# A two-block model on one core: the mixing part of the second block rearranged

## The reference

```
h = x + 0.5 * swiglu(rms(x))
p = rms(h) @ w_in;  u_conv, q, k, v, q_mem = split(p, [768, 1152, 1280, 1408])
y_conv = conv(u_conv)              # a * sigmoid(gate), 31 causal taps per channel
                                   # (384 channels), + bias, layer norm over 384, silu
q, k = rope(rms_per_head(q)), rope(rms_per_head(k))          # 6 and 2 heads of 64
y_swa = softmax(q k^T, own and previous block of 128, with a sink per head) v
mk, mv = split(rms(mem) @ w_mem_kv); mk, q_mem = rms_per_head(mk), rms_per_head(q_mem)
y_mem = softmax(q_mem mk^T) mv                               # 4 heads, 256 rows
h = h + concat(y_conv, y_swa, y_mem) @ w_out
x = rms(h + 0.5 * swiglu(rms(h)))
```

## Time and profile before

| | us |
|---|---|
| median of three runs | 5424.01 |
| the profiled execution, its own time | 5434.72 |
| its span in the profile | 5432.9 |
| PE busy | 5007.7 (92%) |
| DVE busy | 1701.7 (31%) |
| ACT busy | 1048.4 (19%) |
| POOL busy | 153.0 (3%) |
| mean granted clock of PE, share of 2.4 GHz | 0.939 |

### The profile page before, as it was taken

One profiled execution on the slowest core, in us unless ns is written; L12 is line 12 of the kernel. 1 busy time (PEld: TensorE's weight loads), 2 busy tenths in 40 slices (PEclk: granted clock), 3 DMA queues, 4 the chain that ended last, 5 costly groups with the idle time before them and its releaser, 6 DMA issues.

```text
span 5432.9 us, 60219 instructions
## 1 busy us (share of the span) xinstructions
PE 5007.7 (92%) x26216; PEld 2632.1 (48%) x26216; DVE 1701.7 (31%) x3322; ACT 1048.4 (19%) x2280; POOL 153.0 (3%) x139
## 2 busy tenths in 40 slices
PE   7978999997989999988999999959999999959998
PEld 4554555553446667643443444424444444424443
DVE  3253111116146666532112112562113111562112
ACT  1042000001035555512001000151001000151000
POOL 0000000000000000000000000050000000050000
PEclk8999999998978998889999999959999999959999
DMA  5300222210100000021221221201221222201220
GB/s 211 147 17 31 78 109 78 109 62 33 41 1 3 2 3 3 2 102 62 78 78 65 77 78 70 85 9 62 78 74 74 77 78 71 92 16 62 78 74 27
DMA packets 26855, 338.45 MB, mean 62 GB/s; under 512 B 3008, under 2 KB 3008, under 8 KB 6752
## 3 DMA queue, kind: packets, MB, share of 16 engines
q1 hardware_dynamic: 23904, 324.51, 15.9%
q0 software_dynamic: 2688, 10.09, 0.5%
HBM read 330.40 MB, written 4.19 MB: 62 GB/s over the span
## 4 chain that ended last, share of the span: by engine, by line
PE 66%; issue 25%; DVE 4%; ACT 3%; POOL 1%; DMA 0%; SPq 0%; POOLq 0%; DVEq 0%; ACTq 0%
PE ps L872 50%; PE ps L1203 2%; PE ps L899 1%; PE ps L1175 1%; PE ps L1134 1%; PE ps L1186 1%; PE ps L1265 1%; POOL arena L801 1%; PE ps L918 1%; PE ps L1124 1%; DVE rstd L1767 1%; PE ps L1252 1%; PE ps L1249 1%; PE ps L988 1%; PE ps L1004 1%
## 5 line engine op out<-in xcount | busy, mean ns | idle before, releaser
L872 PE MATMUL ps<-arena 128*128 128x512 f32 (+3 forms) x9728 | 3826.2, 556 | 93.1 <-DVE arena L2049 30.0
L872 PEld LDWEIGHTS ps<-arena 128*128 128x128 f32 x9728 | 1848.0, 191 | 2062.2 <-issue 1629.6
L1556 ACT ACTIVATE square<-arena 128x512 f32<-128x512 f32 x88 | 55.4, 630 | 1250.7 <-DVE arena L2021 1250.7
L1928 DVE TENSOR_TENSOR arena<-ps,arena 128x512 f32<-128x512 f32 (+1 forms) x136 | 87.7, 645 | 644.7 <-PE ps L872 644.7
L2021 DVE TENSOR_TENSOR arena<-ps,rstd 128x512 f32<-128x512 f32 x88 | 60.8, 691 | 501.4 <-PE ps L872 501.3
L1940 DVE TENSOR_TENSOR arena<-arena,ps 128x384 f32<-128x384 f32 (+1 forms) x96 | 57.5, 599 | 498.9 <-ACT arena L1478 498.9
L1478 ACT ACTIVATE arena<-ps 128x384 f32<-128x384 f32 (+1 forms) x96 | 50.5, 526 | 797.4 <-PE ps L872 797.4
L801 POOL TENSOR_TENSOR arena<-arena 128x512 f32<-128x512 f32 x120 | 143.9, 1228 | 1787.1 <-ACT arena L1400 1787.1
L2026 DVE TENSOR_TENSOR arena<-ps,arena 128x512 f32<-128x512 f32 x88 | 60.9, 692 | 403.3 <-PE ps L872 403.2
L1348 ACT ACTIVATE square<-arena 128x512 f32<-128x512 f32 (+2 forms) x86 | 61.0, 713 | 525.5 <-PE ps L899 224.2
L899 PE MATMUL ps<-square,ones 128*128 128x512 f32 x220 | 99.7, 598 | 51.6 <-ACT square L1348 45.8
(11 more groups left out here) (256 smaller groups left out, 3631.0 us busy)
## 6 DMA issues: line engine op xcount, KB each, us to landing
arena<-in_panels SPq DMA_DIRECT2D x145, 2048.0 KB, 7.7
arena<-in_panels SPq DMA_DIRECT2D x9, 1536.0 KB, 6.4
arena<-in_bias POOLq DMA_DIRECT2D x8, 512.0 KB, 6.4
arena<-in_x_in SPq DMA_DIRECT2D x1, 3072.0 KB, 11.2
x_save<-arena POOLq DMA_DIRECT2D x1, 2048.0 KB, 7.5
arena<-x_save POOLq DMA_DIRECT2D x1, 2048.0 KB, 28.7
out_x<-arena SPq DMA_DIRECT2D x8, 256.0 KB, 2.2
arena<-in_mem_in POOLq DMA_DIRECT2D x1, 1024.0 KB, 30.6
```

The lines of the kernel that those rows point to most:

```text
L872: ins = pe.matmul(dest, left(k), right(k), start=(k == 0), stop=(k == nk - 1))
L1928: dve.tensor_tensor(Y[:, c, a:b], bank, Y[:, c, a:b], ALU.add).then_inc(sem("tile_free"), one("tile_free"))
```

## The change

The columns of `w_in` are packed in another order: the six convolution tiles (each group and its gate) come first, then q, k and q_mem, then v. The panels keep their sizes.

Taps. DVE now does groups 0 and 1, 48 of its 62 taps in `mix_in` and 2 a step in the first 8 steps of attention. ACT and POOL do group 2, all in `mix_in`, with two product buffers.

Head norms. Squares are used as weights of a matmul with a 2-column operand, so that the sums stand with tokens on partitions (128 x 8 values for a chunk); variance, root and reciprocal are taken there. ACT spreads each value over 64 columns, PE transposes back (four transposes into bank 5), and DVE multiplies. Each item is spread over the following tiles.

Layer norm. The sum, the centring, the squares (into Y), the second sum and the variance move into attention, to steps 9 to 13. In attention the copy of output i-3 goes ahead of score(i). `conv` keeps root, reciprocal, scaling and silu, with the bias inside the sigmoid and the product. PE has no `conv`. In w_out PE first accumulates k = 3 to 7 of four tiles and then waits for the convolution's chunks.

```diff
-        add(np.concatenate([q[:, 0], q[:, 1], q[:, 2], w[:, 1152:1280]], 1))
-        add(np.concatenate([w[:, 1408:1664], conv[:, 0], gate[:, 0]], 1))
-        add(np.concatenate([conv[:, 1], gate[:, 1], conv[:, 2], gate[:, 2]], 1))
+        add(np.concatenate([conv[:, 0], gate[:, 0], conv[:, 1], gate[:, 1]], 1))
+        add(np.concatenate([conv[:, 2], gate[:, 2], q[:, 0], q[:, 1]], 1))
+        add(np.concatenate([q[:, 2], w[:, 1152:1280], w[:, 1408:1664]], 1))
...
+        CONV_TILES, HEAD_TILES = 6, 6
+        MIX_STEPS = CONV_TILES + HEAD_TILES + LAT // P
+        HEAD_ITEMS = {6: [0], 7: [1, 2], 8: [3], 9: [4], 10: [5], 11: [6], 12: [7]}
+        ROPED = range(2, 6)
...
+        DVE_TAPS = {2: 4, 3: 6, 4: 6, 5: 7, 6: 7, 7: 3, 8: 3, 9: 3, 10: 3, 11: 3, 12: 3}
+        POOL_TAPS = {6: 4, 7: 5, 8: 5, 9: 5, 10: 5, 11: 5, 12: 2}
+        PAIR_TAPS = 2
+        LN_MEAN, LN_CENTRE, LN_SQUARES, LN_VAR = 9, 10, 12, 13
...
 POOL (called from mix_in, no longer from attention)
+                for tap in range(1, TAPS):
+                    pool.wait_ge(sem("tap_product"), TAPS * l + tap + 1)
+                    if tap > 1:
+                        pool.wait_ge(sem("pool_tap"), base + tap - 1)
+                    pool.tensor_tensor(y, y, tap_product[tap % 2], ALU.add).then_inc(sem("pool_tap"), one("pool_tap"))
 PE attention, behind scores(i)
+                    if l is not None and i == LN_MEAN:
+                        pe.wait_ge(sem("tapped"), l + 1)
+                        row_sum(lambda c: conv_y[:, c, :])
+                    if l is not None and i == LN_SQUARES:
+                        pe.wait_ge(sem("ln_square"), 3 * (l + 1))
+                        row_sum(lambda c: Y[:, c, 0:LAT])
 PE project (w_out)
+                    for m in range(4):
+                        banks.append(tile())
+                        for k in range(3, KD):
+                            pe.matmul(banks[m], w[:, k, m * P:(m + 1) * P], src[:, k, 0:LAT], start=(k == 3), stop=False)
+                    for m in range(4):
+                        for c in range(3):
+                            if m == 0:
+                                pe.wait_ge(sem("convolved"), more("convolved"))
+                            ins = pe.matmul(banks[m], w[:, c, m * P:(m + 1) * P], src[:, c, 0:LAT], start=False, stop=(c == 2))
 PE mix_in, behind the tile of step s
+                    for it in HEAD_ITEMS.get(s, ()):
+                        pe.wait_ge(sem("head_square"), base + it + 1)
+                        if base + it - 1 > 0:
+                            pe.wait_ge(sem("head_var"), base + it - 1)
+                        for t in range(item_width(it) // P):
+                            ins = pe.matmul(ps[:, stat_bank(it), 2 * t:2 * t + 2], square[:, it % 2, t * P:(t + 1) * P],
+                                            head_ones[:, 0:P:C], start=True, stop=True)
+                    for it in HEAD_ITEMS.get(s - 1, ()):
+                        pe.wait_ge(sem("head_spread"), base + it + 1)
+                        for t in range(item_width(it) // P):
+                            ins = pe.transpose(ps[:, 5, t * P:(t + 1) * P], item_spread(it)[:, t * P:(t + 1) * P], ident)
+                    for it in HEAD_ITEMS.get(s - 2, ()):
+                        if it in ROPED:
+                            pe.matmul(ps[:, 6, :], rotate, item(it), start=True, stop=True)
 ACT mix_in, step s
+                    for it in HEAD_ITEMS.get(s - 1, ()):   # root, wait for head_inverse, spread
+                    if s < CONV_TILES and s % 2 == 1:      # sigmoid of the gate
+                    for it in HEAD_ITEMS.get(s, ()):       # wait for the copied tile, square
+                    for _ in range(POOL_TAPS.get(s, 0)):
+                        conv_tap(l, tap)                   # tap > 2: waits for pool_tap of tap - 2
 DVE mix_in, step s: copy of tile s-1; variance (items of s-1); multiply (items of s-2);
 reciprocal (items of s-1); RoPE (items of s-3); next_taps(l, DVE_TAPS.get(s, 0))
 DVE attention, step i: normalise(i-1); copy output i-3; score(i); then
+                        if i < LN_MEAN - 1:
+                            next_taps(l, PAIR_TAPS)
+                        elif i == LN_MEAN - 1:
+                            last_taps(l)
+                        elif i == LN_CENTRE:
+                            centre(l)
+                        elif i == LN_VAR:
+                            ln_variance(l)
 ACT attention, step i, ahead of the turned copy
+                    if l is not None and i == LN_CENTRE:
+                        for c in range(3):
+                            act.wait_ge(sem("centred"), 3 * l + c + 1)
+                            act.activation(Y[:, c, 0:LAT], conv_y[:, c, :], ACT.Square)
```

More of the change, by code:

```diff
@@ L1009, in attention, with row_sum @@
                 n["unit"] += len(pairs)
+            def row_sum(row):
+                for c in range(3):
+                    ins = pe.matmul(ps[:, 5, :], ones[:, :], row(c), start=(c == 0), stop=(c == 2))
+                ins.then_inc(sem("ln_sum"), one("ln_sum"))
             def project(count, segs, src, dest, ready):
@@ L1417, in attention @@
                 for i in range(len(pairs) + 1):
-                    if l is not None and i >= 1:
-                        for tap in range(TAPS * (i - 1) // TAP_STEPS, min(TAPS, TAPS * i // TAP_STEPS)):
-                            conv_tap(l, tap)
+                    if l is not None and i == LN_CENTRE:
+                        for c in range(3):
+                            act.wait_ge(sem("centred"), 3 * l + c + 1)
+                            act.activation(Y[:, c, 0:LAT], conv_y[:, c, :], ACT.Square).then_inc(
+                                sem("ln_square"), one("ln_square"))
                     if i >= 1:
@@ L1693, in conv @@
+                n["tile"] += 4 + CONV_TILES + HEAD_TILES + LAT // P
             def conv(l):
-                act.wait_ge(sem("tapped"), more("tapped"))
-                n["plain_sums"] += 3
-                n["var"] += 1
-                squares(lambda c: conv_y[:, c, :], 3, 0, LAT, lambda c: act.wait_ge(sem("centred"), more("centred")))
+                act.wait_ge(sem("ln_var"), l + 1)
+                act.activation(rstd[:, 0:LAT], rstd[:, 0:LAT], ACT.Sqrt).then_inc(sem("ln_std"), one("ln_std"))
@@ L1884, in attention @@
                             normalise(i - 1, h)
+                    if i >= 3:
+                        dve.wait_ge(sem("output"), base + i - 2)
+                        dve.tensor_copy(pairs[i - 3]["dest"], ps[:, 7, 0:P]).then_inc(sem("attended"), one("attended"))
                     if i < len(pairs):
@@ L1887, in attention @@
                     if l is not None:
[L1888 to L1892 removed]
+                        if i < LN_MEAN - 1:
+                            next_taps(l, PAIR_TAPS)
+                        elif i == LN_MEAN - 1:
+                            assert n["tap"] == len(TAP_ORDER) * (l + 1)
+                            last_taps(l)
[3 more added lines that the diff above has]
+                            ln_variance(l)
                 n["unit"] += len(pairs)
```

279 lines of the change are left out of this document (158 added, 121 removed).

## The result

The changed kernel takes **5256.9 us** (median of 4, 5256.1 to 5259.8) beside 5422.8 (5421.4 to 5435.5) for the kernel before on the same chip: 0.969 of it, interval 0.9673 to 0.9707. The profiled execution took 5257.3 (span 5255.5); profile against profile the gain is 177.4.

A forecast was written before the change was run, and what follows sets the result against it. It took TensorE to bound mixing and w_out, and a chain attention and conv. 119.5 + 82 + 0 = 201.5 us a layer against 262.5 and 261.3: gain 121, from median 5424.0 to 5303 us, range 5276 to 5328.

The forecast's parts named there:

- mixing: Mixing stage: TensorE's busy time rises from 113.3 to 118.0, its waits mostly go; 119.5 us a layer, bounds 117 and 131.
- second block's attention: Second block's attention: pairs, entry and drain 69.5 us plus layer norm 12.6, so 82 us a layer against 120.3.
- conv: Convolution's norm: remaining chain of about 9.5 us hides beside w_out's first 40 passes; 0 instead of 21.8 us.
- w_out: Output projection: same passes and the same low clock at its beginning, so 54.9 us stays.
- Attention, taps of two channels gone: Second block's attention without ACT and POOL taps: pair cycle of 4.0 us with two DVE taps, 69.5 us in all.
- memory pairs: Second block's attention: eight pairs without sinks, 2.8 us each by TensorE at 1.2 GHz, 22.4 us together.
- the norm: Layer norm's first half inside second block's attention: row sums, late exponential and variance add 12.6 us, bounds 6 and 16.
- Rival (c): Everything better: attention at 2.4 GHz 70 us, norm 6, mixing 117; gain 75 a layer, 5274 us; chance 0.05.
- (b): Mixing: DVE and POOL exclude each other at full price, 131 us a layer; 5326, at most 5350 us; chance 0.12.
- (d): Mixing: small sums and turns make TensorE wait and its clock fall to 1.2 GHz; slower, 5500 us; chance 0.03.
- Rival (a): Second block's attention: pairs stay long at 1.2 GHz without overlap, norm costs 16; 100 us, gain 41 a layer; chance 0.2.
- Rival (e): Attention held by something beside the taps: pairs stay near 6 us, conv's 21.8 moves in; 5415 to 5424; chance 0.05.

The follow-up runs named there:

- e1: Kernel before, with DVE's copy of output i-3 moved ahead of the scores of pair i in the first block's attention alone; 5407.8 us, ratio 0.9957.
- e2: Changed kernel with the copy put back behind the scores in the first block's attention alone; 5270.2 us, ratio 0.9703.
- e3: Kernel before, unchanged, profiled once more for a second trace; 5416.0 us in one run.
- e13: e10 plus 11 products per layer that nobody reads, 512 columns wide, in steps 0 to 6 of the second block's attention; 5242.7 us, ratio 0.9661.
- e5: Kernel before without the 60 ACT products and 60 POOL additions of convolution taps beyond tap 0; 5386.4 us, ratio 0.9924.
- e12: Kernel before with the copy of output i-3 ahead of the scores in both blocks, taps as they were; 5367.6 us, ratio 0.9892.
- e8: Changed kernel without the layer norm's row sums, centring and squares in attention, variance a constant; 5248.2 us, ratio 0.9675.
- e7: Changed kernel with POOL's 60 tap additions only 2 of 512 columns wide, all waits kept; 5255.4 us, ratio 0.9682.
- e4: Changed kernel with w_out waiting for all three convolution chunks, then running its tiles over k = 0 to 7; 5280.4 us, ratio 0.9718.
- e6: Changed kernel with the copy put back behind scores and taps in the second block's attention alone; 5293.9 us, ratio 0.9752.
- e9: e8 with the six row sum products per layer put back on rows that are ready, so nothing waits; 5252.0 us, ratio 0.9673.
- e10: Changed kernel with its layer norm spread singly over attention steps 9 to 17, full result computed; 5244.4 us, ratio 0.9658.

## Why the prediction was wrong

Profile to profile, from the windows above and those of the earlier trace rows (w_out for equal work, as above); "more" is gain beyond the forecast.

| | forecast gain | measured | more |
|---|---|---|---|
| mixing, 2 layers | 1.5 | 7.1 | 5.6 |
| second block's attention, 2 layers | 76.0 | 95.1 | 19.1 |
| conv | 43.3 | 43.3 | 0 |
| w_out, for equal work | 0 | 5.5 | 5.5 |
| first block's attention | 0 | 24.2 | 24.2 |
| all else | 0 | 2.2 | 2.2 |

**The step that failed** is the part "Attention, taps of two channels gone". It read the moved copy as a term of 0.28 us in the second block's DVE cycle ("the copy, which is now ahead of the score"). But `attention` is one function for both blocks, and the first block's share was put at nothing without a reason. There, with no taps, the move alone takes off 20 to 24 us (e1, e2, e3). The forecast used that block's window for its clock and never asked what TensorE waited for in it; the groups of L1004 in the trace of before show the wait, 28.2 us of idle time ahead of the outputs in that stretch, some 27 of it ended by the copy (L1892):
```profile
L1004 PE MATMUL ps<-square,arena 128*64 128x128 f32 x324 | 28.6, 279 | 15.1 <-DVE arena L1892 14.6 <-ACT square L1415 0.5
...
L1004 PE MATMUL ps<-arena 128*64 128x128 f32 x100 | 13.4, 281 | 13.1 <-DVE arena L1892 12.8 <-ACT square L1415 0.3
```
With the 24 us, 5303 would have been 5279, just inside the range. That is not all of it: e2, without that gain, still lies 6 us under the low end, because of the terms below.

**Attention of the second block, 82 forecast, 72.4 measured.** The pairs with two taps were near: 4.0 and 3.5 against 3.77 and 3.37, DVE's pace as said (e13). The late copy's share was not seen, though the trace of before shows TensorE waiting 44.8 us for it in this stage (the line under e5): the prediction gave the whole gain to the chain of taps, while that chain and the copy hold about 21 us each (e5, e12). The end came out near because it was built from the new cycle and not from what leaves. The mis-sized terms are the memory pairs and the norm, and they belong together. A pair was priced at 2.8 for 1.2 GHz; at that level it takes 3.45 (e8), at 2.4 GHz 2.25. That the stage without the norm was met all the same (69.5 forecast, 71.3 and 71.9 in e8) is partly luck: eight memory pairs at 3.45 are 5.2 us above the 22.4 of the sum, and the rest came out some 3 us below. The norm was priced at 12.6; it costs 8.6 in place, and as the clock rises with its row sums, 0.6 to 1.1 in all (72.5 and 72.4 against 71.9 and 71.3). Rival (c), "clock at 2.4 GHz in attention", had 70 us and a chance of 0.05; its weight was too low; the 0.97 of the earlier trace rows, a like stage, spoke for it.

**Mixing, 119.5 forecast, 116.7 measured.** TensorE's busy time was put at 118.0 and is 113.9: the small sums and turns added 0.6 us in layer 0 and 2.3 in layer 1, not 4.7. The clock and the absence of waits were right. DVE beside POOL was right in size: 77 busy (81 forecast), 9.4 of it from the additions (e7), and they cost the stage 1.6 of its length, as much as the 1.5 taken. Rivals (b) and (d) are out.

**conv** was right: hidden fully, the first passes of w_out unbroken, and 9.7 to 11.2 us per layer if not (e4; 9.5 forecast, TensorE's wait 8.8). **w_out** was put at no change. Missed was that it runs at 1.00 from its start when TensorE comes to it straight from attention, and not from 22 us of conv (clock 0.95) or from the 8.8 us wait of e4: 2.8 us a layer.

Rival (a), pairs that stay longer at 1.2 GHz, is half seen in e6 and e8; its own terms give a gain of 42 to 43 a layer where it says 41, which changes nothing here. Rival (e) was right in one point: something beside the taps did hold attention.

## What to carry to other kernels

Before a price is set on a moved instruction, list every call of the function that it stands in, and look in each for what waits for it: a copy of 0.28 us, behind other work in its engine's queue, held 20 to 24. And list an engine's longest waits in the stage before naming what paces it: the copy stood there with 44.8 us. Where TensorE is at 1.2 GHz and busy throughout, a wide product placed among narrow ones can shorten the stage that it is added to (e9 against e8, 2.5 and 1.7 us); where another engine sets the pace, the clock buys nothing (e13). And a wait of several microseconds seen in a trace is worth its length only if the state behind it, the clock above all, stays the same without it.

## What the hardware showed that was not expected

- TensorE, busy 3.00 of 3.00 us over 39 us with passes of 128 and 256 columns, stayed at 0.50 (e8); with single products of 512 columns between the same passes it went to 1.00 and stayed (e10). What exactly raises it was not settled; in e6 the same code kept 1.00 in one layer and lost it in the other, and transposes are among e8's passes, so that their part in it was not told from the width's.
- The same RWKV scan takes 637, 640, 641 or 646 us in different executions, at mean clocks of 0.92 to 0.90. What chooses is open.
- 30 additions of GpSimd, 1.20 us each on the average, lengthen VectorE's work beside them by 9.4 us, a third of a microsecond each; with additions two columns wide the surplus is gone.
